# Half of x1's gate-stage products and its last three gate inputs stand beside c0's second gather tile

## The chip, the cores and the metric

The kernel runs on one core of one Trainium2 chip. The metric is the device time of one execution in microseconds (us), as the median of several runs. The engines of the core are named as in the profile: PE (TensorE matmul), PEld (its weight loads), DVE (VectorE), ACT (ScalarE), POOL (GpSimd) and SP (SyncE, which here only starts weight transfers).

## The reference, cut to what matters

Two blocks follow each other on 256 tokens of width 1024. The change lies in the first, which has two layers over two streams, the main stream x and the context ctx. One layer mixes tokens in three gated branches and then adds a mixture of looked-up experts:

```python
def _token_mix(h, lp, ang, kv_ctx):
    z = h @ lp["w_in"]
    cq, ckv, kr, zf, zp, zg = jnp.split(z, SPLITS, axis=-1)
    ...                                   # attention over 8 heads gives att
    y_a = att @ lp["w_oa"]
    y_b = _fourier_mix(zf) @ lp["w_ob"]
    y_c = _pool_mix(zp, lp["w_grp"], lp["pool_scale"]) @ lp["w_oc"]
    g = jax.nn.sigmoid((zg + lp["b_gate"]).astype(jnp.float32)).astype(h.dtype)
    g_a, g_b, g_c = jnp.split(g, N_BRANCH, axis=-1)
    return (g_a * y_a + g_b * y_b + g_c * y_c) @ lp["w_out"], (k, v)

def _peer(h, w_pq, peer_keys, peer_down, peer_up):
    ...                                   # 128 experts per token are chosen
    a = jnp.einsum("tkd,td->tk", peer_down[ee], hh)
    act = (gg * jax.nn.gelu(a)).astype(hh.dtype)
    return jnp.einsum("tk,tkd->td", act, peer_up[ee])
```

In the last layer the context is used only for its keys and values, so there the context has no mixing and no experts of its own.

## The kernel before, in words

The program calls its four passes c0, x0, x1 and c1: context or main stream, layer 0 or 1 (c1 is the context's keys and values for layer 1). The work is cut into stages such as ("gpre", "x1", 3, 0), and the functions `beside_x0`, `beside_c0` and `order` write the list of them by hand. Each engine walks the same list and issues its own part of every stage, so the list is the order on PE, DVE, ACT and SP alike. There is no scheduler; engines wait on semaphores only.

**The gathers.** Every pass but c1 looks up 128 experts for each token. A tile is 128 tokens (t = 0 or 1), and its 128 lookups go in 16 groups of 8. For one lookup POOL issues an indirect transfer of a 128 x 1024 tile from the table `peer_down` (L2504), DVE multiplies it with h and sums (L1984, `down`), the small gelu chain follows (DVE L1988 to L2003, ACT L1492), ACT writes a diagonal matrix (L1488, `diags`), POOL fetches the row of `peer_up` into the same buffer (L2504), and PE adds it up in four 128 x 128 by 128 x 512 passes (L992, `up`). For c0 the loop in `gather` does this: in group n, PE does `up(n - 1)`, DVE `down(n)`. The eight buffers `rows` are used in turn for a down row and an up row.

**Stages beside a gather.** A tile has 32 slots, two for each group. The stages in an even slot are run by PE ahead of `up(n - 1)`, by DVE between `down(n)` and `act_of(n)`, by ACT between `diags(n - 1)` and `tanh(n)`. In c0's second tile slot 32 is group 0, so slots 32 to 42 carry x1's branches (Fourier, pooling, queries) in groups 0 to 5, and slots 44, 46 and 48 carry ("gpre", "x1", dp, 0) in groups 6, 7 and 8. From slot 50 on, groups 9 to 15, the slots are empty. Runs of groups with empty slots are written as a hardware loop (`groups`), here six turns; POOL has its own loops, which the stages don't touch.

**Gates and branch products.** For each quarter dp of the 1024 columns and each branch j (0 attention, 1 Fourier, 2 pooling), `gpre` multiplies hT with a 1024 KB chunk of wG on PE (16 matmuls, L879) and ACT takes the tanh (L1449) into a place that `gate_at` names. `gate` with part 3 multiplies one 1024 KB chunk of wO with the branch outputs on PE (L899: 8 matmuls for j = 0, 4 for j = 1, 4 for j = 2), and DVE weights each with its gate and adds up (L1852, L1855, L1857) into mixT. The gates for dp = 0 to 2 of x1 are made beside the gathers of c0; those for dp = 3 and all the y products are made behind them.

**Between the gathers.** After c0's last tile nothing is gathered until x1's own experts are chosen. In that stretch stand: the norm of c1, the three gpre of dp = 3, the transposes of c1 (L697), its projection (L711), kv (L728, L736, L746), the heads of x1 (L846, L856, L869), the four gate stages, `out_` (L711), norm and transposes of x1, and the scoring (L922, L932).

**Weights.** SP starts the weight chunks in the order of the stages, into a ring of three buffers `wring`: a chunk is started when the chunk three before it has been used (`chunks`, L2309). Loads of a norm's gain stand in the same queue (L2315).

## Time and profile before

| | us |
|---|---|
| median of 3 runs | 4159.94 |
| lowest and highest of them | 4153.65, 4164.02 |
| the profiled execution, its own time | 4160.42 |
| its span in the profile | 4158.6 |
| c0's second gather tile (first `up` to the end of the last) | 1731.7 to 2103.2 |
| stretch without a gather, to the first expert row of x1 | 2103.2 to 2345.8 |

The times in a profile run from the start of the span. PE is busy for 83% of it, DVE for 56%, POOL for 36%, ACT for 23%. In the timeline a row gives start, duration, engine, line and operation, and in brackets how long the engine had been idle and what ended that. The program's fp32 matmuls appear as two records each, so 16 matmuls are x32.

### The profile page before, as it was taken

What the parts mean: (1) busy time and instruction counts of PE and PEld (TensorE: products, weight loads), DVE (VectorE), ACT (ScalarE), POOL (GpSimd) and SP (SyncE); (2) the same over time, 40 slices, a digit from 0 to 9 for tenths busy, and PEclk for the clock granted to TensorE, in tenths of its full rate; (3) what the DMA queues carried; (4) which work ended last, traced back from release to release, by engine and by line L of the source; (5) the groups of instructions that cost most, each with busy time, mean ns of one, the idle gap of its engine ahead of it and who ended that gap; (6) DMA issues with size and microseconds to landing.
All of it is one profiled execution on the core that took longest, in us unless ns stands there. A gap on an engine that the chain in (4) does not pass through costs nothing.

```text
span 4158.6 us, 43344 instructions
## 1 busy us (share of the span) xinstructions
PE 3469.0 (83%) x14118; PEld 2193.7 (53%) x14118; DVE 2323.3 (56%) x4974; ACT 950.0 (23%) x1940; POOL 1509.0 (36%) x1757
## 2 busy tenths in 40 slices
PE   6999787888895887777688677767789979999999
PEld 2576443354462452333255522222259869798898
DVE  2313876444557776444423666666546676565564
ACT  1301111121111111221121111111123453334443
POOL 0000566555555666566600277667730000000000
PEclk8999899999997998898899899989999989999999
DMA  6575899989897999999922599989965414545444
GB/s 269 192 267 194 316 391 367 363 313 345 343 359 292 388 394 360 333 375 374 352 102 96 209 388 400 381 335 379 399 255 186 177 55 165 185 175 179 143 175 153
DMA packets 273452, 1156.77 MB, mean 278 GB/s; under 512 B 30849, under 2 KB 31617, under 8 KB 234370
## 3 DMA queue, kind: packets, MB, share of 16 engines
q0 software_dynamic: 221184, 805.40, 51.0%
q1 hardware_dynamic: 52098, 349.23, 22.8%
q8 instruction: 90, 1.47, 0.1%
q14 instruction: 80, 0.66, 0.0%
HBM read 1153.47 MB, written 1.05 MB: 278 GB/s over the span
## 4 chain that ended last, share of the span: by engine, by line
PE 50%; DMA 19%; issue 11%; DVE 11%; POOL 7%; ACT 2%; POOLq 0%; SPq 0%; DVEq 0%; ACTq 0%
DMA rows<-in_peer_up,iup 11%; PE ps L992 11%; DMA rows<-in_peer_down,idown 7%; PE ps L1045 7%; PE ps L1047 7%; PE ps L1046 7%; POOL rows L2504 4%; PE ps L711 3%; PE ps L879 3%; PE ps L922 3%; POOL rows L2439 3%; DVE rows L1984 2%; PE ps L899 2%; DVE rows L1933 1%; PE ps L951 1%
## 5 line engine op out<-in xcount | busy, mean ns | idle before, releaser
L992 PE MATMUL ps<-rows,diag 128*128 128x512 f32 x2048 | 968.0, 631 | 292.6 <-DMA rows<-in_peer_up,iup 287.9
L992 PEld LDWEIGHTS ps<-rows,diag 128*128 128x128 f32 x2048 | 405.9, 202 | 835.7 <-issue 593.0
L1984 DVE CUSTOM_DVE_ANT_0 rows<-rows,ps 128x1024 f32<-128x1024 f32 x512 | 615.0, 1220 | 413.7 <-DMA rows<-in_peer_down,idown 405.7
L951 PE MATMUL ps<-rows,diag 128*128 128x512 f32 x1024 | 511.7, 625 | 209.8 <-DMA rows<-in_peer_up,iup 159.5
L2504 POOL DMA_INDIRECT rows<-in_peer_down,idown x512 | 488.6, 954 | 400.4 <-PE ps L992 281.9
L2504 POOL DMA_INDIRECT rows<-in_peer_up,iup x512 | 483.3, 944 | 257.0 <-issue 110.6
L951 PEld LDWEIGHTS ps<-rows,diag 128*128 128x128 f32 x1024 | 176.6, 191 | 542.8 <-DMA rows<-in_peer_up,iup 365.8
L1045 PE MATMUL ps<-hT_hi,w_hi 128*128 128x256 f32 x1600 | 452.4, 283 | 8.9 <-DVE hT_lo L2095 8.9
L1047 PE MATMUL ps<-hT_lo,w_hi 128*128 128x256 f32 x1600 | 453.1, 283 | 0.0
L1046 PE MATMUL ps<-hT_hi,w_lo 128*128 128x256 f32 x1600 | 451.3, 282 | 0.0
L1933 DVE CUSTOM_DVE_ANT_0 rows<-rows,ps 128x1024 f32<-128x1024 f32 x256 | 309.2, 1220 | 210.7 <-DMA rows<-in_peer_down,idown 209.1
L2568 POOL TENSOR_TENSOR ss<-nwt,minus_half 128x1 f32<-128x1 f32 x24 | 13.2, 550 | 1076.2 <-DVE nwt L1716 1076.2
L1488 ACT ACTIVATE diag<-ident,act 128x128 f32<-128x128 f32 x768 | 261.2, 395 | 459.7 <-PE ps L992 381.4
L2085 DVE TENSOR_TENSOR w_lo<-wring,w_hi 128x2048 fp32r<-128x2048 f32 x120 | 274.7, 2291 | 114.6 <-ACT w_hi L1559 113.6
L1045 PEld LDWEIGHTS ps<-hT_hi,w_hi 128*128 128x128 f32 x1600 | 306.1, 191 | 10.9 <-issue 10.8
L1046 PEld LDWEIGHTS ps<-hT_hi,w_lo 128*128 128x128 f32 x1600 | 305.6, 191 | 0.1
L1047 PEld LDWEIGHTS ps<-hT_lo,w_hi 128*128 128x128 f32 x1600 | 304.9, 191 | 0.0
L2439 POOL DMA_INDIRECT rows<-in_peer_down,idown x256 | 243.0, 949 | 122.9 <-issue 58.3
L2439 POOL DMA_INDIRECT rows<-in_peer_up,iup x256 | 242.5, 947 | 100.0 <-issue 72.0
L1559 ACT ACTIVATE w_hi<-wring 128x2048 fp32r<-128x2048 f32 x120 | 229.2, 1911 | 116.6 <-DMA wring<-in_wdn 86.5
L1492 ACT ACTIVATE th<-g 128x8 f32<-128x8 f32 x96 | 20.0, 208 | 833.5 <-DVE g L1943 539.5
L879 PE MATMUL ps<-hT,wring 128*128 128x256 f32 x928 | 207.8, 383 | 1.4 <-ACT hT L1304 1.4
(315 smaller groups left out, 4298.2 us busy)
## 6 DMA issues: line engine op xcount, KB each, us to landing
wring<-in_wgu SPq DMA_DIRECT2D x66, 1024.0 KB, 4.7
wring<-in_wdn SPq DMA_DIRECT2D x33, 1024.0 KB, 4.8
wring<-in_wG SPq DMA_DIRECT2D x29, 1024.0 KB, 7.9
rows<-in_wmod SPq DMA_DIRECT2D x27, 1024.0 KB, 7.9
wring<-in_wpq SPq DMA_DIRECT2D x24, 1024.0 KB, 4.9
rows<-in_wgu SPq DMA_DIRECT2D x22, 1024.0 KB, 4.8
wring<-in_wmod SPq DMA_DIRECT2D x21, 1024.0 KB, 7.2
rows<-in_peer_down,idown POOLq DMA_INDIRECT x768, 6.4
```

What stands on the lines that cost most here:

```text
L879: last = pe.matmul(b[:, dt * TOK:(dt + 1) * TOK], w[:, k * 256 + dt * P:k * 256 + (dt + 1) * P], hT[:, k, :], start=(k == 0), stop=(k == K ...
L951: ins = pe.matmul(ps[:, UPB + half, :], diag[:, j % DIAGS, :], rows[:, s, half * 512:(half + 1) * 512], start=(first and j == 0), stop=(la ...
L992: ins = pe.matmul(ps[:, UPB + half, :], diag[:, j % DIAGS, :], rows[:, j, half * 512:(half + 1) * 512], start=(first and j == 0), stop=(la ...
L1045: pe.matmul(out_, lh[l_at], rh[r_at], start=start, stop=False, skip_group_check=skip)
L1046: pe.matmul(out_, ll[l_at], rh[r_at], start=False, stop=False, skip_group_check=skip)
L1047: return pe.matmul(out_, lh[l_at], rl[r_at], start=False, stop=stop, skip_group_check=skip)
L1488: act.activation(diag[:, j % DIAGS, :], ident[:, :], ACT.Copy, scale=act8[:, j:j + 1]).then_inc(diag_ready, 1)
L1933: dve.tensor_tensor_reduce(out=rows[:, s, :], in0=rows[:, s, :], in1=h_ps, scale=1.0, scalar=0.0, op0=ALU.mult, op1=ALU.add, accum_out=a8[ ...
L1984: dve.tensor_tensor_reduce(out=rows[:, j, :], in0=rows[:, j, :], in1=h_ps, scale=1.0, scalar=0.0, op0=ALU.mult, op1=ALU.add, accum_out=a8[ ...
L2085: dve.tensor_tensor(W2_LO[c % SLOTS2], w, W2_HI[c % SLOTS2].bitcast(f32), ALU.subtract).then_inc(lo_ready, 1)
L2439: pool.indirect_dma_start(out=rows[:, s, :], out_offset=None, in_=table, in_offset=bass.IndirectOffsetOnAxis(ap=offs, axis=0)).then_inc(ro ...
L2504: pool.indirect_dma_start(out=rows[:, j, :], out_offset=None, in_=table, in_offset=bass.IndirectOffsetOnAxis(ap=offs[:, j:j + 1], axis=0)) ...
```

## The change

The change puts seven stages into the empty even slots 50 to 62 of c0's second tile. Four are new stages ybc: for one dp they make the y products of j = 1 and 2 and weight and add them on DVE. Three are the gpre of dp = 3, which stood behind the gather. Gate, for x1 alone, keeps only j = 0 and one addition. The chunk of wO is loaded in two halves, columns 1024 to 2047 for ybc and 0 to 1023 for gate. Since more gates are alive at once, those of dp = 3 go where already used ones were, and a new mark mixBC orders that: ACT waits for the ybc that has read the old gate before it writes the new one.

```diff
@@ beside_c0
     place(32, branches("x1") + [("gpre", "x1", dp, 0) for dp in range(3)], 2)
+    place(50, [("ybc", "x1", 0), ("ybc", "x1", 1), ("gpre", "x1", 3, 1), ("gpre", "x1", 3, 2), ("ybc", "x1", 3), ("ybc", "x1", 2), ("gpre", "x1", 3, 0)], 2)
@@ order
-    o += k[0:1] + [("gpre", "x1", 3, j) for j in range(3)] + k[1:] + flat(heads("x1") + mixing("x1") + scoring("x1"))
+    o += k + flat(heads("x1") + mixing("x1") + scoring("x1"))
@@ MARKS
+    "mixBC": (4, ["x1"]),
@@ chunks_of
     if name == "gate":
+        if st[1] == "x1":
+            return [("wO", (l, st[2], slice(None), slice(0, SLOT_W // 2)), SLOT_W // 2)]
...
+    if name == "ybc":
+        return [("wO", (l, st[2], slice(None), slice(SLOT_W // 2, SLOT_W)), SLOT_W // 2)]
@@ gate_at
             if dp == 3:
-                return (mb[:, 0:512], mb[:, 512:D], zA[0].rearrange("p t n -> p (t n)")[:, 0:512])[j]
+                return (junk[:, 512:D], h[0][:, 0, 512:D], h[0][:, 1, 512:D])[j]
@@ PE
+                branch_products(run, dp, [0] if run == "x1" else [0, 1, 2], 0)
...
+            def ybc(run, dp):
+                if dp == 0:
+                    at_evac(pe, ("Y", run))
+                    at_evac(pe, ("G", run))
+                branch_products(run, dp, [1, 2], 4)
@@ ACT, gpre
+                if run == "x1" and dp == 3:
+                    at_mark(act, "mixBC", run, (4, 1, 2)[j])
@@ DVE
             def gate(run, dp, part_):
...
+                if run == "x1":
+                    key = ("y", run, dp, 0)
+                    at_evac(dve, ("g", run, dp, 0))
+                    m = mixT[:, 2 * dp:2 * dp + 2, :]
+                    release(dve.scalar_tensor_tensor(m, pair_of(gate_at(run, dp, 0)), 1.0, pair_of(at_mm(dve, key)), ALU.add, ALU.mult), key)
+                    at_evac(dve, key)
+                    dve.tensor_tensor(m, m, pair_of(gate_at(run, dp, 1)), ALU.add).then_inc(mark["mixT"], 1)
+                    return
...
+            def ybc(run, dp):
+                kept = pair_of(gate_at(run, dp, 1))
+                tmp = pair_of(zA[0].rearrange("p t n -> p (t n)")[:, 0:512])
+                for j in (1, 2):
+                    key = ("y", run, dp, j)
+                    at_evac(dve, ("g", run, dp, j))
+                    release(dve.scalar_tensor_tensor(kept if j == 1 else tmp, pair_of(gate_at(run, dp, j)), 1.0, pair_of(at_mm(dve, key)),
+                                                     ALU.add, ALU.mult), key)
+                    at_evac(dve, key)
+                no = (0, 1, 3, 2).index(dp) + 1
+                dve.tensor_tensor(kept, kept, tmp, ALU.add).then_inc(mark["mixBC"], 1)
+                at_mark(dve, "mixBC", run, no)
```

On PE, at the end of c0's second tile and in the stretch behind it, the program before reads (L992 is `up`, L879 gpre, L697 and L711 c1's transposes and projection; the loop is shortened):

```order
L879 MATMUL ps<-hT,wring 128x256 x16
L992 MATMUL ps<-rows,diag 128x512 x16
L599 UNCONDITIONAL_BRANCH
...
L599 COMPARE_AND_BRANCH
L992 MATMUL ps<-rows,diag 128x512 x32
L648 MATMUL ps<-mrows,sel 128x512 x6
L879 MATMUL ps<-hT,wring 128x256 x48
L697 MATMUL ps<-ident,h_ctx 128x128 x16
L711 MATMUL ps<-wring,hT 128x416 x16
```

And changed, with its own line numbers (L1009 is `up`, L885 gpre, L910 the y products, L703 and L717 c1's):

```order
L885 MATMUL ps<-hT,wring 128x256 x16
L1009 MATMUL ps<-rows,diag 128x512 x16
L910 MATMUL ps<-YT,wring 128x256 x4
L910 MATMUL ps<-ypT,wring 128x256 x4
L1009 MATMUL ps<-rows,diag 128x512 x16
...
L885 MATMUL ps<-hT,wring 128x256 x16
L1009 MATMUL ps<-rows,diag 128x512 x32
L654 MATMUL ps<-mrows,sel 128x512 x6
L703 MATMUL ps<-ident,h_ctx 128x128 x16
L717 MATMUL ps<-wring,hT 128x416 x16
```

The loop is gone, a stage stands ahead of each of the last seven `up` pieces (the last of them the gpre in front of the closing x32), and the 48 matmuls between the norm's small ones and c1's transposes are gone.

On SP's queue, from the gain of a norm in that tile to c1's projection weights, before and changed:

```order
L2315 DMA gain<-in_norm_g 128x1024
L2309 DMA wring<-in_wG 128x2048 x3
L2309 DMA wring<-in_wA 128x1664 x2
L2309 DMA wring<-in_wukv 128x1024
L2309 DMA wring<-in_wO 128x2048 x4
```

```order
L2350 DMA wring<-in_wO 128x1024 x2
L2350 DMA wring<-in_wG 128x2048 x2
L2350 DMA wring<-in_wO 128x1024 x2
L2350 DMA wring<-in_wG 128x2048
L2356 DMA gain<-in_norm_g 128x1024
L2350 DMA wring<-in_wA 128x1664 x2
L2350 DMA wring<-in_wukv 128x1024
L2350 DMA wring<-in_wO 128x1024 x4
```

The four half chunks of ybc are new in the queue ahead of the gain of c1's norm, which now stands behind seven chunks.

## Rows read from the trace of the kernel before

**Rows 1.** The page, part 4: the chain that ended last, by engine
```profile
PE 50%; DMA 19%; issue 11%; DVE 11%; POOL 7%; ACT 2%; POOLq 0%; SPq 0%; DVEq 0%; ACTq 0%
```
**Rows 2.** That chain in c0's second tile and behind it: start us, us, what
```profile
1756.21 3.69 PE ps L992 x4
...
2049.86 3.67 PE ps L992 x4
...
2059.48 5.61 DMA rows<-in_peer_down,idown
2065.11 1.22 DVE rows L1984
...
2067.58 6.38 DMA rows<-in_peer_up,iup
...
2110.81 22.88 PE ps L879 x96
...
2204.05 27.88 PE ps L899 x128
```
**Rows 3.** Timeline of PE in c0's second tile
```profile
1756.21 15.70 PE L992 MATMUL ps<-rows,diag 128*128 128x512 f32 x32 [3.13 <-DMA rows<-in_peer_up,iup]
...
1833.82 16.17 PE L992 MATMUL ps<-rows,diag 128*128 128x512 f32 x32 [6.02 <-DMA rows<-in_peer_up,iup]
1849.83 7.07 PE L879 MATMUL ps<-hT,wring 128*128 128x256 f32 x32
...
1905.10 15.70 PE L992 MATMUL ps<-rows,diag 128*128 128x512 f32 x32 [1.86 <-DMA rows<-in_peer_up,iup]
1929.51 16.11 PE L992 MATMUL ps<-rows,diag 128*128 128x512 f32 x32 [8.72 <-DMA rows<-in_peer_up,iup]
...
2074.01 29.28 PE L992 MATMUL ps<-rows,diag 128*128 128x512 f32 x64 [8.48 <-DMA rows<-in_peer_up,iup]
```
**Rows 4.** Busy time by stretch, three groups of that tile
```profile
core 0: us, PE busy (x) PEld busy (x) DVE busy (x) ACT busy (x) POOL busy (x), PEclk, DMA share, GB/s
1858.40:1881.60 23.20, 21.17 (x65) 11.98 (x65) 10.16 (x19) 4.14 (x11) 15.16 (x17) 1.00 1.02 408
...
1929.50:1953.70 24.20, 16.16 (x33) 6.85 (x33) 10.38 (x20) 3.21 (x8) 15.08 (x18) 0.85 0.94 341
...
1756.20:1783.10 26.90, 20.45 (x56) 10.88 (x56) 14.07 (x40) 5.79 (x15) 17.54 (x21) 0.88 0.95 355
```
**Rows 5.** Timeline of DVE, from one group's last step to the next group's first
```profile
2050.69 0.17 DVE L2003 TENSOR_TENSOR act<-g,gates 128x8 f32<-128x8 f32 x1 [0.22 <-DVE g L1998]
2060.02 1.22 DVE L1984 CUSTOM_DVE_ANT_0 rows<-rows,ps 128x1024 f32<-128x1024 f32 x1 [9.16 <-DMA rows<-in_peer_down,idown]
```
**Rows 6.** Weight transfers from 2103 to 2280 us: count, KB each, us to landing
```profile
wring<-in_wO SPq DMA_DIRECT2D x4, 1024.0 KB, 4.8
...
wring<-in_wA SPq DMA_DIRECT2D x2, 832.0 KB, 4.4
...
wring<-in_wukv SPq DMA_DIRECT2D x1, 512.0 KB, 3.3
```
**Rows 7.** Timeline of PE between the gathers
```profile
2136.81 11.41 PE L711 MATMUL ps<-wring,hT 128*128 128x416 f32 x32 [1.40 <-ACT hT L1304]
...
2234.92 17.01 PE L711 MATMUL ps<-wring,shared 128*128 128x512 f32 x32
...
2252.91 14.00 PE L711 MATMUL ps<-wring,shared 128*128 128x512 f32 x32
...
2282.43 20.96 PE L922 MATMUL ps<-hT,wring 128*128 128x256 f32 x96 [0.99 <-ACT hT L1304]
```
**Rows 8.** Timeline of DVE between the gathers
```profile
2116.88 0.69 DVE L1774 TENSOR_TENSOR h_ctx<-h_ctx,ps 128x512 f32<-128x512 f32 x1
...
2209.61 0.69 DVE L1852 SCALAR_TENSOR_TENSOR shared<-h_in,ps 128x512 f32<-128x512 f32 x1 [1.07 <-PE ps L899]
...
2277.02 0.69 DVE L1774 TENSOR_TENSOR h_in<-h_in,ps 128x512 f32<-128x512 f32 x1
```

More of the change, by code:

```diff
@@ L890, in gate, with branch_products @@
                         at_evac(pe, ("pv", run, n))
-                    at_evac(pe, ("Y", run))
-                    at_evac(pe, ("G", run))
+                    if run != "x1":
+                        at_evac(pe, ("Y", run))
+                        at_evac(pe, ("G", run))
+                branch_products(run, dp, [0] if run == "x1" else [0, 1, 2], 0)
+            def branch_products(run, dp, js, k0):
                 w = chunk()
-                for j, ks in enumerate(([0, 1, 2, 3], [4, 5], [6, 7])):
+                for j in js:
+                    ks = ([0, 1, 2, 3], [4, 5], [6, 7])[j]
                     b = job(("y", run, dp, j))
@@ L898, in gate @@
                             rhs = attT[:, k, :] if j == 0 else (YT, ypT)[j - 1][:, (k % 2) * TOK:(k % 2 + 1) * TOK]
-                            last = pe.matmul(b[:, dt * TOK:(dt + 1) * TOK], w[:, k * 256 + dt * P:k * 256 + (dt + 1) * P], rhs,
+                            last = pe.matmul(b[:, dt * TOK:(dt + 1) * TOK], w[:, (k - k0) * 256 + dt * P:(k - k0) * 256 + (dt + 1) * P], rhs,
                                              start=(k == ks[0]), stop=(k == ks[-1]))
@@ L902, in gate @@
                 chunk_end()
+            def ybc(run, dp):
+                if dp == 0:
+                    at_evac(pe, ("Y", run))
+                    at_evac(pe, ("G", run))
+                branch_products(run, dp, [1, 2], 4)
             def out_(run, half, c):
@@ L1280, in _ @@
                        "start": start, "mod": mod, "norm": norm, "hT": hT_, "zA": zA_, "kv": kv, "zF": zF, "four": four, "q": q_, "att": att,
-                       "gate": gate, "gpre": gpre, "out": out_, "pq": pq, "gather": gather, "fb": fb, "fin": fin}
+                       "gate": gate, "gpre": gpre, "ybc": ybc, "out": out_, "pq": pq, "gather": gather, "fb": fb, "fin": fin}
             def run_stages(stages):
@@ L2280, in _ @@
             program = {"pre": pre, "hT2": hT2, "gu": gu, "dn": dn, "cout": cout, "qkv": qkv, "ao": ao, "post": post, "cin": cin, "ln": ln, "moba": moba,
-                       "start": start, "mod": mod, "norm": norm, "kv": kv, "q": q_, "att": att, "gate": gate, "out": out_, "route": route,
+                       "start": start, "mod": mod, "norm": norm, "kv": kv, "q": q_, "att": att, "gate": gate, "ybc": ybc, "out": out_, "route": route,
                        "gather": gather, "fin": fin, "final": final, "lower": lower}
@@ L2320, in per_stage @@
                     return int(args[1] == 2)
-                return {"mod": 2, "zA": 1, "zF": 1, "four": 2 - args[-1] if name == "four" else 0, "gate": 1, "gpre": 1, "out": 1}.get(name, int(name == "pq" and args[1] < 8))
+                return {"mod": 2, "zA": 1, "zF": 1, "four": 2 - args[-1] if name == "four" else 0, "gate": 1, "gpre": 1, "ybc": 1, "out": 1}.get(name, int(name == "pq" and args[1] < 8))
             for name, *args in STAGES:
```

## The prediction

> **What bounds the kernel now.** I read the chain that ended last first, since it says whose time counts: half of it is PE's, a fifth is transfers, DVE and issue have 11% each [rows 1]. Then I followed the same chain through the two places that the change touches, because its shares mix stages with different limits.
>
> In c0's second tile the chain goes round once for each group: PE takes the first rows, that frees a buffer, a down row is fetched (5.61 us), DVE takes it (1.22), an up row is fetched (6.38), and only then can PE begin the next group [rows 2]. The timeline of PE shows what that leaves. An empty group is some 16 us of `up` and then 8 to 9 us of idle, ended by the up row [rows 3]. From 1905.10 to 2074.01 there are seven such groups, so one takes 24.13 us. So PE has a hole in each, and work in it is paid only where it outlasts the hole or slows the round trip.
>
> Behind the gather there is no such cover. The three gpre take 22.88 us of the chain and the four gate stages 27.88 us, all PE's [rows 2]. The stretch ends with the scoring, which the next gather waits for; all that is taken out of it comes off the total, if nothing else is late instead.
>
> **Part 1, the three gpre.** They are 48 matmuls, 22.88 us of chain. Not all of it comes back, because they cover the norm of c1. DVE begins the first h piece that c1's transposes wait for at 2116.88 [rows 8], six microseconds into the gpre. What is late next is that norm. How long the way from that piece to a running matmul is, the same code shows on x1: the piece begins at 2277.02 [rows 8], the matmuls behind the transposes at 2282.43 [rows 7], 5.41 us later, with a PE that had stood idle before, as it now will here. So c1's projection starts at 2116.88 + 5.41 = 2122.29 where it now starts at 2136.81 [rows 7]. **Saved: 14.5 us.** Its bounds are 22.9 (the norm would not count) and 11.5 (the projection loses 3 us to a low clock, below). Its weights are not late: SP's queue has them behind the last gpre's chunk, and the ring frees their buffers in groups 13 and 14, before the gather ends. The same holds for the gain of c1's norm, which goes out when the gpre of group 12 is done, some 100 us before DVE wants it.
>
> **Part 2, the gate stages.** The 64 matmuls take 27.88 us; j = 0 is 8 of every 16, so 13.94 us remain. **Saved: 13.9 us.** The end is as before: PE waits for DVE's product and one addition. For one quarter DVE now has one product and one addition of 0.69 us each [rows 8] against 3.5 us of PE, so it keeps up. The weights shrink with the work: three half chunks are in the ring early, the fourth starts when the first is used, 3.5 us into the stage, and is wanted at 10.5; a whole chunk took 4.8 us [rows 6]. The first chunk of `out_` starts 7 us into the stage and is wanted at about 16.
>
> **Part 3, what the gather pays.** PE gets four ybc of 8 matmuls (27.88 / 128 x 16 records = 3.5 us each) and three gpre of 7.07 [rows 3], 35 us of work in seven holes of 8 to 9 us. The nearest rows are groups 6 to 8 of the same tile, which have a gpre and one 1024 KB chunk each: three of them take 1905.10 - 1833.82 = 71.28, or 23.76 each, less than the 24.13 of an empty one [rows 3]. The windows say why. With the gpre the granted clock is 1.00 (the 2.4 GHz level throughout), without it 0.85 [rows 4]: behind 8.7 us of idle the first row of `up` takes 3.67 us in the chain [rows 2]. So a gpre gives back some 0.4 to 0.9 us, although the transfers are slower beside its chunk. A ybc leaves 5 us of hole. After 3.13 us of idle the clock had already fallen once, the first row took 3.69 [rows 2, 3], so I give it no gain, and 0.3 us of loss for its chunk. Three gpre at -0.7 and four ybc at +0.3 make **-1 us**. The bounds for the seven: -0.9 each (23.20 against 24.13), -6; and +2.8 each, as in the group at 1756.20, which had two chunks at once and took 26.90 [rows 4], +19.6.
>
> DVE gets three operations of 0.69 us in a ybc, 2.1 us and some waiting, between `down` and `act_of`. Queued behind them are the last two small steps, on which ACT's diagonals and so PE's next-but-one piece depend. They are covered: DVE sits idle for 9.16 us after these steps [rows 5], and the diagonals are held back by PE's own progress, not by DVE. The products that ybc waits for are made at the start of PE's hole, while DVE is still at its down rows. ACT's new wait on mixBC stands ahead of its tanh for the gelu; the ybc it names lies one group back or more, so it costs nothing. If that cover is gone, it is the third rival below. POOL issues what it issued. That the six loop turns become straight code I cost at nothing: groups 0 to 8 are straight code and no slower.
>
> The transfers are nearer to their limit. The tile takes 4 x 512 + 2 x 832 + 512 = 4224 KB more [rows 6], 4.3 MB: ybc's half chunks of wO, and c1's weights that now come early. But never more than 1024 KB in a group, as in groups 6 to 8. These move 408 GB/s at a share of 1.02, an empty one 341 [rows 4]. The tile has that room by the rows. The Trainium skill, DMA: Bandwidth & Descriptors, section Where 436 GB/s comes from, speaks against the change: it puts the limit from HBM at some 358 GB/s for a core, by which 4.3 MB more would take 12 us. The trace disagrees with it in the group at 408, so the sum goes by the rows.
>
> **The sum.** 14.5 + 13.9 + 1 = 29.4 us off 4160.4 of the profiled execution (span 4158.6 and 1.8 around it) is **4131.0**. That execution lies 0.5 us above the median of the runs, which is nothing here.
>
> **The rivals.**
> *The transfers are full.* Each extra byte lengthens the tile at the rate of an empty group: 4.3 MB at 341 GB/s is 12.7 us, which gives 4160.4 - 28.4 + 12.7 = 4144.7. For it: the share is 0.94 even in empty groups, and the group with two chunks took 2.8 us more. Against it: three groups with a chunk each took less time, not more. The skill's 358 GB/s, above, would be this case.
>
> *The clock falls in the stretch behind.* c1's transposes now follow 7 us of idle. In the present trace the first half of `out_` took 17.01 us and the second 14.00 for the same work [rows 7], after a short idle. One such loss is 3 us (4134), a projection wholly at the lower level would lose its own 11.4 us again (4142). Against the latter: x1's scoring came up at full pace directly behind its transposes [rows 7].
>
> *A stage is serial with its group.* Were PE's stage, DVE's three operations and the way to the diagonals in the round trip, each stage would cost its own length: 4 x (3.5 + 2.1) + 3 x 7.07 = 43.6 us, the total 4160.4 - 28.4 + 43.6 = 4175.6, slower than before. It decides from 28.4 / 7 = 4.1 us for each stage. Against it speak the gpre groups (7.07 us of work, no loss) and DVE's 9.16 us of idle; for it only that no c0 group of this tile has had work of PE and DVE in a chain with the gelu.
>
> *The change does less than it says.* If c1's norm were later than it looks, or another wait took the gates' place, one of the two savings halves: 4138.
>
> **How the numbers follow.** The forecast, 4125 to 4137, has 0.66; full transfers 0.12; a low clock 0.09; less than it says 0.07; the serial stage 0.03; more gain in the gather than I count (down to 4160.4 - 28.4 - 6.3 = 4125.7, and some of the norm's cover) 0.03. The range 4122 to 4146 takes in all but the serial stage, the heaviest end of full transfers and a wholly low clock on top of another loss. A measurement of this kernel can tell about 0.3%, 12.5 us, from no change. Faster by more than that is below 4147.5, which all cases but the serial stage and the worst of the transfers reach: 0.93. Within it 0.05, slower 0.02.
>
> **What would show it.** In the changed profile PE should reach c1's projection 19 us after the end of the last `up` (33.5 now), hold 64 records of y products between the heads and `out_` in 14 us, and show groups 9 to 14 of the tile at 23 to 25 us. If these groups stand at 26 with DMA at a share of 1.0 throughout, the transfers were full. If PE waits there for diagonals of ACT, the stage is serial. A projection above 12 us means the clock. The prediction is wrong if groups cost over 2 us more each, or if PE waits for a chunk in the gate stages.

## The result, and the profile after the change

The change made the kernel faster: 4136.62 us against 4159.54 us, medians of 7 runs each on one chip, ratio 0.9948 with a 95% interval of 0.9934 to 0.9961. That is 21.6 us off at the ratio, 16 to 27.5 by the interval. Forecast were 29.4 us and 4131.0; the result lies inside the range of 4122 to 4146, 5.6 us from the forecast. The gain of 29.4 us that was forecast lies just above the interval of the measured one. The profiled execution took 4140.86 us, its span 4138.7 against 4158.6. The page, part 1, busy time of the engines after the change:

```profile
PE 3472.4 (84%) x14118; PEld 2195.5 (53%) x14118; DVE 2322.5 (56%) x4974; ACT 950.1 (23%) x1940; POOL 1518.8 (37%) x1757
```

The work was only moved, so these totals say little. Where the time came from stands in the timelines. First PE in c0's second tile (start us, us, engine and line, operation, count, and in brackets the idle time before and what ended it):

```profile
1880.20 14.22 PE L1009 MATMUL ps<-rows,diag 128*128 128x512 f32 x32 [0.85 <-DMA rows<-in_peer_up,iup]
...
1902.72 5.42 PE L1009 MATMUL ps<-rows,diag 128*128 128x512 f32 x12 [1.39 <-DMA rows<-in_peer_up,iup]
...
1917.73 1.89 PE L910 MATMUL ps<-YT,wring 128*128 128x256 f32 x8
1919.45 1.89 PE L910 MATMUL ps<-ypT,wring 128*128 128x256 f32 x8
1927.13 15.79 PE L1009 MATMUL ps<-rows,diag 128*128 128x512 f32 x32 [5.79 <-DMA rows<-in_peer_up,iup]
...
1952.10 16.95 PE L1009 MATMUL ps<-rows,diag 128*128 128x512 f32 x32 [5.72 <-DMA rows<-in_peer_up,iup]
...
1976.80 5.42 PE L1009 MATMUL ps<-rows,diag 128*128 128x512 f32 x12 [0.84 <-DMA rows<-in_peer_up,iup]
...
2001.02 5.40 PE L1009 MATMUL ps<-rows,diag 128*128 128x512 f32 x8 [2.30 <-DMA rows<-in_peer_up,iup]
...
2028.91 16.10 PE L1009 MATMUL ps<-rows,diag 128*128 128x512 f32 x32 [6.50 <-DMA rows<-in_peer_up,iup]
...
2055.24 16.59 PE L1009 MATMUL ps<-rows,diag 128*128 128x512 f32 x32 [6.77 <-DMA rows<-in_peer_up,iup]
2071.66 7.07 PE L885 MATMUL ps<-hT,wring 128*128 128x256 f32 x32
2080.00 27.86 PE L1009 MATMUL ps<-rows,diag 128*128 128x512 f32 x64 [1.26 <-DMA rows<-in_peer_up,iup]
```

The holes that had 8 to 9 us of idle [rows 3] now hold the moved products (3.6 us for a ybc, 7.07 for a gpre). From the start of one `up` to the next the seven groups take 24.4, 25.0, 24.7, 24.2, 27.9, 26.3 and 24.8 us, in the order ybc 0, ybc 1, gpre, gpre, ybc 3, ybc 2, gpre. That is 177.3 us where the same seven took 168.9 [rows 3]: **+8.4**, and the two groups of ybc 3 and ybc 2 have 6.0 of it. The two groups ahead of the seven took 2.4 us less and the closing 64 records 1.4 less (27.86 against 29.28, PE comes warm, that is at the full granted clock, out of a gpre). "The fifth group" and the like count from here on among these seven. Busy time in four of the groups (columns as in [rows 4]):

```profile
1902.70:1927.10 24.40, 17.72 (x48) 8.96 (x48) 11.45 (x25) 3.63 (x10) 16.34 (x19) 0.94 1.02 408
...
1976.80:2001.00 24.20, 21.18 (x64) 11.99 (x64) 10.58 (x21) 4.36 (x12) 15.41 (x19) 1.00 0.99 378
2001.00:2028.90 27.90, 19.68 (x48) 9.42 (x48) 12.79 (x27) 3.63 (x10) 17.14 (x21) 0.89 1.00 377
2028.90:2055.20 26.30, 19.56 (x48) 9.83 (x48) 12.02 (x24) 3.42 (x9) 15.71 (x19) 0.89 0.95 354
```

The group that moved most bytes a second (408) is not the long one. SP's transfers around the fifth and sixth group:

```profile
1998.75 0.33 SPq L2350 DMA_DIRECT2D wring<-in_wG  x1
1999.12 0.43 SPq L2356 DMA_DIRECT2D gain<-in_norm_g  x1
2022.44 26.39 SPq L2350 DMA_DIRECT2D wring<-in_wA  x2
```

The last row holds two transfers, at 2022.44 and 2048.50. A gpre frees its chunk at the end of its hole, a ybc in the middle of its own, so the last wG chunk (1024 KB), the gain (512 KB) and the first wA chunk (832 KB) fall into the fifth group, 2.4 MB. Then PE between the gathers, same columns:

```profile
2107.79 1.13 PE L654 MATMUL ps<-mrows,sel 2*128 2x512 f32 x4
...
2122.19 3.48 PE L703 MATMUL ps<-ident,h_ctx 128*128 128x128 f32 x16 [10.48 <-DVE h_ctx L1793]
2126.61 11.41 PE L717 MATMUL ps<-wring,hT 128*128 128x416 f32 x32 [0.95 <-ACT hT L1321]
...
2193.98 14.05 PE L910 MATMUL ps<-shared,wring 128*128 128x256 f32 x64 [0.78 <-ACT shared L1321]
2209.61 1.12 PE L654 MATMUL ps<-mrows,sel 2*128 2x512 f32 x2 [1.58 <-DVE shared L1871]
2210.66 15.68 PE L717 MATMUL ps<-wring,shared 128*128 128x512 f32 x32
...
2257.22 23.25 PE L939 MATMUL ps<-hT,wring 128*128 128x256 f32 x96 [0.99 <-ACT hT L1321]
```

PE now waits 10.48 us for DVE's norm of c1 and then begins the projection 18.8 us after the gather's last `up` (2126.61 - 2107.79), where it took 33.6 (2136.81 - 2103.22). The gate products are 64 records in 14.05 us, with no wait for a chunk, and 15.6 us (2209.61 - 2193.98) stand where 29.5 stood. The projection is at the full pace of 11.41 us. x1's scoring takes 23.25 us against 20.96 [rows 7], 2.3 us given back at a lower clock.

In one sum, after minus before, in these two executions: seven groups +8.4, the two ahead -2.4, the closing block -1.4, to c1's projection -14.8, the gates -13.8, the first half of `out_` -1.3 (15.68 against 17.01) and -0.3 in the small matmuls ahead of it, x1's norm +0.4, the scoring +2.3, what follows it +0.2. With +0.1 between projection and gates that puts x1's first expert row 22.7 us earlier, and 2.8 are lost in the rest of the program, which the change does not touch: -19.9 in the span.

### The profile page after: what moved, and what is told of

It reads as the page before. It is cut to its first block, busy times and chain, and to the rows that moved or that the text cites. A ratio compares the mean times of both kernels' runs of the same rounds, so it can differ in the third digit from the quotient of the medians.

```text
span 4138.7 us, 43250 instructions
## 1 busy us (share of the span) xinstructions
PE 3472.4 (84%) x14118; PEld 2195.5 (53%) x14118; DVE 2322.5 (56%) x4974; ACT 950.1 (23%) x1940; POOL 1518.8 (37%) x1757
## 3 DMA queue, kind: packets, MB, share of 16 engines
q1 hardware_dynamic: 52674, 349.23, 22.9%
## 4 chain that ended last, share of the span: by engine, by line
PE 49%; DMA 18%; issue 12%; DVE 10%; POOL 8%; ACT 2%; POOLq 0%; SPq 0%; DVEq 0%; ACTq 0%
DMA rows<-in_peer_up,iup 11%; PE ps L1009 11%; PE ps L1062 7%; PE ps L1063 7%; PE ps L1064 7%; DMA rows<-in_peer_down,idown 6%; POOL rows L2545 6%; PE ps L717 3%; PE ps L939 3%; PE ps L885 3%; POOL rows L2480 2%; DVE rows L2025 2%; PE ps L968 1%; PE ps L910 1%; DVE rows L1974 1%
## 5 line engine op out<-in xcount | busy, mean ns | idle before, releaser
L1009 PE MATMUL ps<-rows,diag 128*128 128x512 f32 x2048 | 967.7, 631 | 262.5 <-DMA rows<-in_peer_up,iup 256.4
L1009 PEld LDWEIGHTS ps<-rows,diag 128*128 128x128 f32 x2048 | 404.7, 202 | 803.6 <-issue 535.2
L885 PE MATMUL ps<-hT,wring 128*128 128x256 f32 x928 | 206.0, 380 | 1.4 <-ACT hT L1321 1.4
```

Source lines behind the costliest of these rows:

```text
L885: last = pe.matmul(b[:, dt * TOK:(dt + 1) * TOK], w[:, k * 256 + dt * P:k * 256 + (dt + 1) * P], hT[:, k, :], start=(k == 0), stop=(k == K ...
L1009: ins = pe.matmul(ps[:, UPB + half, :], diag[:, j % DIAGS, :], rows[:, j, half * 512:(half + 1) * 512], start=(first and j == 0), stop=(la ...
```

## The experiments

Of the three terms two fit within 0.3 us. Open was the third: why do the seven groups take 177 us, when three gpre groups before them take 23.76 each? The theories that the runs were to tell apart:

- **B, bytes.** Each chunk lengthens the gather by its bytes over the DMA rate. (The expectations have B, above all the 2.4 MB of the fifth group, together with G as T.)
- **C, the clock.** A short ybc leaves PE idle long enough that the next `up` starts slow, and so every row behind it is late.
- **G, the gain.** SP issues the transfer of c1's gain right behind the last wG chunk, and it stands in the way of rows.
- **S, straight code.** The loop turns written out cost something.
- **P, the phase**, formed on runs 1 to 8, run 6 above all: the cost depends on when in the group a chunk starts. At the end of its hole PE waits for up rows. A chunk that SP starts early in the hole comes in among these. One that starts when `up` has begun comes in beside down rows, which are paced by PE itself.

Group times in us, from one start of `up` to the next, worked out from each run's timeline of PE; ratios against the kernel before on the same chip, with 95% interval. Runs 1 to 4 had one chip (before 4160.32 us), 5 to 8 another (4251.71), 9 to 11 a third job (4239.02), 12 a fourth (4253.98).

```
                          groups                                     sum    ratio
before (shown)            24.4 24.1 24.3 23.7 24.4 23.9 24.2         168.9
after  (shown)            24.4 25.0 24.7 24.2 27.9 26.3 24.8         177.3  0.9948 [0.9934, 0.9961]
1  after again            25.0 25.9 25.1 22.7 27.4 26.9 25.5         178.5  0.9943 [0.9920, 0.9965]
2  gain early             24.3 25.4 24.9 23.2 27.6 26.9 24.5         176.7  0.9952 [0.9929, 0.9976]
3  ybc twice              23.3 23.4 23.0 22.4 29.3 22.8 22.9         167.1  0.9917 [0.9880, 0.9954]
4  before, straight code  23.6 25.2 24.3 23.6 24.1 24.5 24.0         169.4  1.0004 [0.9992, 1.0016]
5  before, warm           23.9 22.9 23.9 23.4 24.9 23.6 23.4         166.1  0.9992 [0.9974, 1.0010]
6  before, one load       26.5 27.5 27.1 29.4 26.7 26.6 27.0         190.7  1.0055 [1.0038, 1.0072]
7  gain early, late wA    27.9 25.6 23.6 22.8 27.5 24.8 23.9         176.0  0.9949 [0.9922, 0.9975]
8  as 7, ybc twice        24.8 23.5 25.1 23.5 28.0 22.7 23.5         170.9  0.9928 [0.9900, 0.9956]
9  chunk late             24.4 23.8 24.8 22.2 28.6 24.7 23.7         172.1  0.9932 [0.9902, 0.9962]
10 warm, chunk early      24.4 23.0 25.0 23.9 30.0 25.2 23.9         175.3  0.9945 [0.9928, 0.9963]
11 late, reordered        25.2 24.7 23.9 23.9 24.7 23.5 23.0         168.9  0.9942 [0.9927, 0.9957]
12 twice, reordered       24.7 24.0 23.4 23.3 25.2 22.8 24.1         167.5  0.9940 [0.9923, 0.9957]
```

The groups of different jobs are not quite alike. In runs 1 to 4, and in the traces of before and after, a chunk freed by a gpre left 0.6 to 2.3 us ahead of the next `up`. In runs 5 to 12 many such chunks, and some freed by a ybc, left 4 to 6.5 us behind the start of `up` (in run 7, 1934.26 against 1928.08). Why is not known.

**1. The changed kernel again.** No edit.

> The changed kernel once more, to see which group times repeat. In the profile shown, the seven groups with a new stage took 24.4, 25.0, 24.7, 24.2, 27.9, 26.3 and 24.8 us from first up to first up, against 24.13 for each before, +8.4 in all. If the bunched transfers cause the loss (theory T: the last wG chunk, the gain of c1's norm and c1's first wA chunk, 2.4 MB, fall into one group), the 27.9 repeats within 0.7 us, and so does the 26.3. If it is chance in the row transfers, the two long groups move elsewhere.

Measured 4138.48 us. The two long groups are there again (27.4, 26.9), and the sum is 1.2 us from the first trace. They are no accident of one execution, and a difference of some 2 us between two sums is the scatter.

**2. The gain early.** SP loads the gain of c1's norm ahead of ybc 0's chunk:

```diff
-                if name == "norm":
+                if name == "ybc" and args == ["x1", 0]:
+                    load_gain(A["norm1_g"][1])
+                if name == "norm" and args == ["c1", 0]:
+                    pass
+                elif name == "norm":
```

> The gain of c1's norm is loaded ahead of ybc's first chunk, about where the kernel before had it, and no longer beside the last wG chunk. T: the group of 27.9 us loses 2 to 3 us, the others stay; the end of the last up comes 2 to 3 us earlier. Rival C (the clock and PE's hole: a ybc of 3.5 us leaves 5 us of idle, the clock falls, and PE's stage no longer pays for itself): nothing changes, 27.9 stays.

Measured 4138.91 us, groups 27.6 and 26.9: nothing moved. G falls, and with it that half of T.

**3. Each ybc product twice.** The second pass starts from zero again, so the output is the same; the ybc lasts 7.2 us like a gpre, and frees its chunk as late.

```diff
-                    for dt in range(2):
+                    for dt in [0, 1] * (2 if k0 else 1):
```

> Each ybc makes its products twice over in the same banks (the first pass is overwritten), so PE has 7 us of work in the hole, as with a gpre, and the same transfers. Clock theory C: the granted clock in the four ybc groups goes from about 0.90 to 0.97 or more, the first row of up takes 2.0 instead of 3.8 us, and each of these groups gets about 1 us shorter, 4 us in all. Transfer theory T: the four groups stay within 0.4 us each, for the round trip then waits for rows. Serial theory: each gets 3.5 us longer, 14 us in all.

More work of PE made the groups shorter: 167.1 against 178.5, and all but the fifth are at 22.4 to 23.4. That is 11.4 us, where C had forecast 4 and the serial theory 14 us of loss. The timeline of PE in this run, the sixth group and its end, and under it SP's transfer of c1's second weights:

```profile
2021.52 5.42 PE L1009 MATMUL ps<-rows,diag 128*128 128x512 f32 x12 [1.15 <-DMA rows<-in_peer_up,iup]
...
2036.12 3.62 PE L910 MATMUL ps<-YT,wring 128*128 128x256 f32 x16
2039.57 3.62 PE L910 MATMUL ps<-ypT,wring 128*128 128x256 f32 x16
2044.36 14.30 PE L1009 MATMUL ps<-rows,diag 128*128 128x512 f32 x32 [1.17 <-DMA rows<-in_peer_up,iup]
```

```profile
2043.22 0.33 SPq L2350 DMA_DIRECT2D wring<-in_wA  x1
```

The chunk leaves at 2043.22, 1.1 us before `up`, where after's left at 2048.50 and `up` began at 2055.24 (below). PE's `up` then takes 14.30 us (2055.24: 16.59), and the up row ahead of it, in the chain of waits, 5.97 us:

```profile
2038.34 5.97 DMA rows<-in_peer_up,iup
```

The busy time of its second group shows that bytes alone don't lengthen a group: 406 GB/s and 23.40 us.

```profile
1923.50:1946.90 23.40, 21.18 (x64) 11.97 (x64) 12.69 (x25) 3.42 (x9) 15.47 (x18) 1.00 1.01 406
```

The run was not yet decisive, as it changes the clock and the chunk's start together. Of its total, 4119.35 us (span 4117.2 against 4140.0 in run 1), 13.5 us stand at the end of the tile (first small norm matmul at 2094.95 against 2108.45). The rest came in stretches with the same code, and the interval is 0.9880 to 0.9954, so the total is not to be read as the worth of the edit.

**4. Straight code alone.** Before, with seven empty steps in the table, which makes the six loop turns straight code:

```diff
+    place(50, [("nop", "x1")] * 7, 2)
```

> The kernel before with seven empty stages in slots 50 to 62, so that the six loop turns on PE, DVE and ACT become straight code and nothing else changes. If straight code costs something (instruction loading), the seven groups of 24.13 us grow, by 1.2 us each if it were the whole of the loss. I expect no change: 24.1 within 0.3 us each, total within 3 us of the kernel before.

Measured 4161.10 us, ratio 1.0004, groups 169.4 (one of its eight times, 11011.73 us, stands apart, unexplained; the median hardly feels it). S falls; the prediction's zero for it holds.

**5. Work without transfers.** Before, with 16 unused matmuls of the gpre's shape in each of the seven holes:

```diff
+            def warm(run, n):
+                b = job(("warm", n))
+                for dt in range(2):
+                    for k in range(KT):
+                        last = pe.matmul(b[:, dt * TOK:(dt + 1) * TOK], ident[:, :], hT[:, k, :], start=(k == 0), stop=(k == KT - 1))
+                release(last, ("warm", n))
```

> The kernel before, with 16 matmuls of gpre's shape in each of the seven empty groups, on ident and hT, their result unused and no transfer added. Clock theory C: PE's hole is filled, the first row of up takes 2.0 instead of 3.7 us, and each of the seven groups falls from 24.1 to about 22.8, the tile gets 8 to 10 us shorter and the whole kernel with it. Serial theory: each group grows by up to 7 us. If the clock does not count, 24.1 stays.

The sum is 166.1, 0.4 us per group below the 168.9 of the trace of before (another chip), and the total is 4251.73 against 4251.71. C had forecast groups of 22.8 and 8 to 10 us of the total. Timeline of PE and one window:

```profile
1955.02 15.64 PE L993 MATMUL ps<-rows,diag 128*128 128x512 f32 x32 [3.02 <-issue]
1970.50 7.07 PE L1284 MATMUL ps<-hT,ident 128*128 128x256 f32 x32
1977.93 14.00 PE L993 MATMUL ps<-rows,diag 128*128 128x512 f32 x32 [0.36 <-DMA rows<-in_peer_up,iup]
```

```profile
1977.90:2001.80 23.90, 20.91 (x64) 12.08 (x64) 10.40 (x20) 3.20 (x9) 16.53 (x20) 1.00 0.97 355
```

Without idle ahead `up` takes 14.00 us, with 3.02 us of it 15.64. But PE then waits longer for its next rows, so a group wins 0.4 us of these 1.6. C is real and small, on its own. In four of the seven groups the granted clock was 1.00, in the other three 0.93.

**6. A transfer without work.** Before, with one 1024 KB chunk and two tiny matmuls in each hole, so that the chunk is freed, and the next one started, at the very start of the hole:

```diff
+            def load(run, n):
+                chunk()
+                for key in (("load", n, 0),):
+                    b = job(key)
+                    ended(pe.matmul(b[:, 0:16], ident[:, :], ident[:, 0:16], start=True, stop=True), key)
+                    release(pe.matmul(b[:, 0:16], ident[:, :], ident[:, 0:16], start=True, stop=True), key)
+                chunk_end()
```

> The kernel before, with one more wG chunk of 1024 KB loaded and freed in each of the seven empty groups, and no work beside two tiny matmuls. This is the price of a chunk with a cold PE. By C and T together a chunk costs about 1.0 us a group (24.1 to 25.1), 7 us in all, which the warm PE of a gpre group hides. If full transfers bound the tile, each grows by 1 MB at 341 GB/s, 3.1 us, 21 us in all; if transfers are free, 24.1 stays.

The expectation fell: total +23.4 us on 4251.71 (ratio 1.0055), groups of 27.2 in the mean. The 3.1 us a group and 21 in all that it had named for full transfers are what came. Timeline of PE and one window:

```profile
1984.33 16.43 PE L995 MATMUL ps<-rows,diag 128*128 128x512 f32 x32 [10.62 <-DMA rows<-in_peer_up,iup]
2000.59 0.29 PE L1286 MATMUL ps<-ident 128*128 128x16 f32 x2
2011.39 16.55 PE L995 MATMUL ps<-rows,diag 128*128 128x512 f32 x32 [10.29 <-DMA rows<-in_peer_up,iup]
```

```profile
1956.90:1984.30 27.40, 16.81 (x36) 7.48 (x36) 10.59 (x22) 3.42 (x9) 15.30 (x18) 0.75 0.94 345
```

PE waits 10.3 to 10.6 us for its up row, where before it waited 8 to 9. In the fourth group (29.4) SP started the gain as well, right behind the chunk. The six groups with a chunk alone take 26.9 us, 2.8 more than the 24.13 of an empty one [rows 3]; the chunk's 1,048,576 bytes over the 341 GB/s of an empty group [rows 4] are 3.1 us. The rate is that of an empty group too (345), so here B alone would do. The Trainium skill, DMA: Bandwidth & Descriptors, section Issuing engines are not separate DMA queues, says that transfers issued by different engines run on the same 16 DMA engines and interleave; run 6 agrees, with these 2.8 us a chunk. Yet the gpre groups [rows 3] have the same chunk for nothing. What differs, beside PE's clock, is its start: there SP starts it when the gpre has ended, 1 to 2 us ahead of `up`, and here 10.5 to 12.7. From this came P.

**7. Late weights.** Run 2, and SP holds c1's first weights until c0's rows are done:

```diff
+                    if name == "zA" and args == ["c1", 0]:
+                        at_mark(sp, "fin", "c0", 2)
```

> The change with the gain early and with c1's wA and wukv held back on SP until c0's last tile is done, so that these transfers leave the gather's last groups. T: the last ybc group (26.3, 26.9 and 26.9 us in three runs) falls to about 25 and the one with the last gpre by some 0.5; the long one (27.4 to 27.9) by 1, since wA's first chunk starts within it. c1's projection still starts on time, for wA lands some 9 us before it is wanted. Total 3 us less than the change. C alone: the groups stay.

The sixth and seventh groups fell to 24.8 and 23.9, from 26.9 and 25.5 in run 1, as expected: the chunk of wA is what they had paid. The fifth stayed at 27.5, where 1 us less was expected, so neither the gain nor wA makes it long. The first took 27.9, which no theory had; in this trace two chunks of 1024 KB start within it (1934.26 and 1948.36), but in run 6 two do as well (1935.92 and 1946.19) and it took 26.5. The total, 0.9949, is that of the change and not 3 us less: the sum is only 1.3 us under 177.3. c1's projection begins on time, 19.0 us after the gather's last `up` (2150.77 - 2131.75).

**8. Run 7 with each product twice.** Its edit is run 3's on top of run 7's:

```diff
-                    for dt in range(2):
+                    for dt in [0, 1] * (2 if k0 else 1):
```

> The last one with ybc's products made twice, so that PE is warm in all seven groups. C and T: the groups take 23 to 23.5 us but for the long one, the whole lies 3 us under the run with the products twice alone (4119.4), near 4116. If late wA is nothing beside a warm PE, 4119.

The sum is 170.9, between runs 3 and 7; the first and third groups (24.8, 25.1) are above the 23 to 23.5 expected. The fifth stands at 28.0 with PE warm, no gain and no wA in it. Total 4224.80, 0.9928, not below run 3's ratio of 0.9917.

**9. The chunk late, PE unchanged.** The test of P against C: after, where SP waits for the first row of the next `up` before it starts a chunk whose buffer a ybc has freed. PE's work and idle time stay.

```diff
+                    if before in ybc_rows:
+                        sp.wait_ge(upp_done, ybc_rows[before])
```

> The change, with SP starting the chunk that a ybc frees only when PE has done the first row of the next up piece; PE's work and all bytes stay. Phase theory P, formed on the runs so far: a chunk started early in PE's hole gets in front of the up rows for which PE waits, one started late, as behind a gpre or behind products made twice, comes in beside up and costs little. P: the four ybc groups fall to 24 to 24.7 us each (from 24.4 to 27.9, the one behind the last wG chunk to about 26), the seven from 177 to about 171, total 5 to 7 us under the change. Clock theory C: PE is as idle as before, so nothing changes, 177. Bytes alone (T): nothing changes.

The sum is 172.1 (P had 171), 5.2 below the changed kernel's first trace and 6.4 below run 1 (both on another chip), at the same bytes and with PE as cold. But of the 5.2 only 2.1 lie in the four ybc groups, the rest in the gpre groups, of which P says nothing. The fifth group did not fall to 26. The total, 0.9932 with 0.9902 to 0.9962, cannot be told from the change's. SP and PE in this run around the sixth group:

```profile
2071.02 0.33 SPq L2354 DMA_DIRECT2D wring<-in_wA  x1
```

```profile
2042.81 16.30 PE L1011 MATMUL ps<-rows,diag 128*128 128x512 f32 x32 [4.59 <-DMA rows<-in_peer_up,iup]
2058.95 1.89 PE L911 MATMUL ps<-YT,wring 128*128 128x256 f32 x8
2060.67 1.89 PE L911 MATMUL ps<-ypT,wring 128*128 128x256 f32 x8
2067.54 15.70 PE L1011 MATMUL ps<-rows,diag 128*128 128x512 f32 x32 [4.97 <-DMA rows<-in_peer_up,iup]
```

The chunk leaves 3.5 us behind the start of `up`, and PE had waited 4.97 us. In the changed kernel, SP around that group:

```profile
2048.50 0.33 SPq L2350 DMA_DIRECT2D wring<-in_wA  x1
```

It left 6.7 us ahead of `up` (2055.24), and PE had waited 6.77. In the chain of waits of the changed kernel the up row in that hole takes 8.12 us against 6.38 [rows 2]:

```profile
2047.07 8.12 DMA rows<-in_peer_up,iup
```

**10. PE warm, the chunk early.** The counterpart: 8 unused matmuls behind each ybc, when its chunk is already freed.

```diff
                 branch_products(run, dp, [1, 2], 4)
+                b = job(("warm", dp))
+                for k in range(KT):
+                    last = pe.matmul(b[:, 0:TOK], ident[:, :], hT[:, k, :], start=(k == 0), stop=(k == KT - 1))
+                release(last, ("warm", dp))
```

> The change, with 8 matmuls more behind each ybc, on ident and hT and unused, after the chunk has been freed. PE is as warm as with the products made twice, but the chunk still starts early in the hole. P: the seven groups stay near 175 to 177 us, less 0.4 us for each warm piece. C: they fall to 167, as in the run with the products made twice.

The sum is 175.3, where P had 175 to 177 less 0.4 for each warm piece, and C 167. PE and SP around the same group:

```profile
2050.93 14.29 PE L1013 MATMUL ps<-rows,diag 128*128 128x512 f32 x32 [2.94 <-DMA rows<-in_peer_up,iup]
...
2068.51 3.62 PE L922 MATMUL ps<-hT,ident 128*128 128x256 f32 x16
2076.12 15.70 PE L1013 MATMUL ps<-rows,diag 128*128 128x512 f32 x32 [4.00 <-DMA rows<-in_peer_up,iup]
```

```profile
2068.70 0.33 SPq L2354 DMA_DIRECT2D wring<-in_wA  x1
```

The chunk left 7.4 us ahead of `up`, PE still had to wait 4.00 us in spite of the extra work, and the group took 25.2. In the fifth group too the chunk was early (6.4 us ahead). In the first and second it was not. PE and SP there:

```profile
1949.09 14.00 PE L1013 MATMUL ps<-rows,diag 128*128 128x512 f32 x32 [3.53 <-issue]
```

```profile
1930.63 20.99 SPq L2354 DMA_DIRECT2D wring<-in_wG  x2
1977.76 24.30 SPq L2354 DMA_DIRECT2D wring<-in_wO  x2
```

The chunk that ybc 0 freed left at 1951.30 (the second of the first row) and that of ybc 1 at 1977.76, 2.2 and 5.7 us (`up` at 1972.06) behind the start of `up`. So the edit gave an early chunk in two of the four groups only, and that the sum came out as P had it is in part luck: the unexplained fifth group took 30.0. What the runs say of P has to be read group by group. "Early" is 5.5 us and more ahead of `up`, "late" 1.2 us ahead to 6.2 behind; PE is "cold" where a ybc leaves it idle as in the change, "warm" where the hole is filled. In brackets the run (the first values are the trace of the change):

```
                    second group                            sixth group
cold, chunk early   25.0 25.9 (1) 25.4 (2) 25.6 (7)         26.3 26.9 (1) 26.9 (2)
cold, chunk late    23.8 (9) 24.7 (11)                      24.7 (9)
cold, no chunk                                              24.8 (7)
warm, chunk early                                           25.2 (10)
warm, chunk late    23.4 (3) 23.5 (8) 23.0 (10) 24.0 (12)   22.8 (3)
warm, no chunk                                              22.7 (8)
```

In the sixth group an early chunk of 832 KB costs 1.6 to 2.4 us and a late one nothing, with PE cold or warm, and the clock is worth 1.1 to 2.1. Runs 9 and 10, from one job, are the cold late and the warm early corner; by PE's work alone the warm one should be the shorter, and it is 0.5 us longer. In the second group the start is worth 0.3 to 2.1 us. In the first it is not seen outside run 7 (24.3 to 25.0 early, 24.4 and 25.2 late in runs 9 and 11), and in the fifth not at all (28.6 in run 9). The other corners stand in different jobs, one trace each, so these are sizes and no more.

**11. Chunk late, gain early, another order.** As 2 and 9, with the seven steps in the order ybc 0, ybc 1, gpre, gpre, ybc 2, gpre, ybc 3:

```diff
-    place(50, [("ybc", "x1", 0), ("ybc", "x1", 1), ("gpre", "x1", 3, 1), ("gpre", "x1", 3, 2), ("ybc", "x1", 3), ("ybc", "x1", 2), ("gpre", "x1", 3, 0)], 2)
+    place(50, [("ybc", "x1", 0), ("ybc", "x1", 1), ("gpre", "x1", 3, 1), ("gpre", "x1", 3, 2), ("ybc", "x1", 2), ("gpre", "x1", 3, 0), ("ybc", "x1", 3)], 2)
```

> Late chunks as in the run before last, the gain of c1's norm early, and the stages in the order ybc 0, ybc 1, gpre 1, gpre 2, ybc 2, gpre 0, ybc 3, so that a half chunk is started where the change starts the last wG chunk and its group takes 27.9 us. P: the seven groups near 169 us, the total 8 to 10 us under the change, 31 to 33 under the kernel before. If the long group comes from that chunk wherever it is fetched, it moves one group ahead; if it comes from the expert rows of that group, it stays in place.

The sum is 168.9, and the long fifth group is gone (24.7):

```profile
2026.81 5.40 PE L1011 MATMUL ps<-rows,diag 128*128 128x512 f32 x8 [1.86 <-DMA rows<-in_peer_up,iup]
...
2051.47 15.47 PE L1011 MATMUL ps<-rows,diag 128*128 128x512 f32 x32 [5.02 <-DMA rows<-in_peer_up,iup]
```

Neither of the two alternatives came: the last wG chunk, which now starts in front of the fourth group (2001.64 against `up` at 2002.93), took its length nowhere (23.9), and the fifth group, with the same expert rows, is short. The seven groups then pay what they paid before, 168.9, for 35 us more of PE's work and all the bytes. The order ends with a ybc and no longer with a gpre, so the closing block goes back to 29.82 us from 27.86. The total, 0.9942, cannot be told from the change's 0.9948, where 8 to 10 us less were forecast.

**12. Products twice, gain early, the new order.** The edits of 2, 3 and 11's order together; of 9's wait nothing.

```diff
-    ... ("ybc", "x1", 3), ("ybc", "x1", 2), ("gpre", "x1", 3, 0)], 2)
+    ... ("ybc", "x1", 2), ("gpre", "x1", 3, 0), ("ybc", "x1", 3)], 2)
```

> The version to beat both kernels: the gain of c1's norm early, the stages in the order of the run before, and ybc's products made twice, which fills PE's hole and starts each chunk late without a wait on SP. By P the seven groups take 163 to 167 us (177 in the change), none over 25; the total lies 12 to 18 us under the change and 35 to 40 under the kernel before, a ratio of 0.991 to 0.992.

The sum is 167.5, at the upper end of the 163 to 167 expected, and the fifth group 25.2, where none was to be over 25. The total missed its 0.991 to 0.992: 0.9940 with 0.9923 to 0.9957. It beats the kernel before, as the change does, and not provably the change.

## Why the prediction was right, and where it was off

**Right: what bounds the kernel.** PE has a hole in each group and none behind the gather. 36.8 us of the chain's PE work (22.88 and 13.94) went into the holes, and 28.6 (14.8 and 13.8) came off the stretch behind.

**Right: the three gpre.** Forecast -14.5, measured -14.8. The norm of c1 is late next, as said: PE waits 10.48 us for DVE's last h piece. x1's way from piece to matmul carried over, and the 22.9 us that the chain seemed to offer were not to be had.

**Right: the gate stages.** Forecast -13.9, measured -13.8, 14.05 us of products without a wait for a chunk.

**Off: what the gather pays.** The mis-sized term is part 3's four ybc at +0.3 each; they took +0.3, +0.8, +3.8 and +2.2. The three gpre, put at -0.7 each, took +0.6, +0.1 and +0.6. Instead of -1 us the seven groups cost +8.4, of which the groups ahead of them (half chunks in them now) and the closing block gave back 3.8: +4.6 at the end of the tile. Both bounds, -6 and +19.6, held it. So the total is close to the forecast although this term is 5.6 us off. The reasoning that was off is the choice of the nearest row. Groups 6 to 8 of the tile have a chunk each for nothing, and I took the chunk for cheap. Their gpre lasts till the hole's end and so holds the next chunk back (and keeps PE warm). A ybc frees its buffer in the middle of the hole (1921.37, the hole ends at 1927.13). From this the prediction's "never more than 1024 KB in a group" is wrong too: 2.4 MB start in or just ahead of the fifth. What the runs show of the excess: of the sixth group's +2.2 an early start is worth 1.6 to 2.2 (run 9, and run 7 without the chunk), and the second group falls to 23.8 and 24.7 with its chunk late (runs 9 and 11). The +3.8 of the fifth and the +1.3 of the three gpre are not explained by it. The half chunk of ybc itself, the only cost I counted, was the wrong one: the transfer that a ybc lets start is that of a later stage. (The first row of 3.67 us, read in part 3 as behind 8.7 us of idle, stands behind 8.19; nothing hangs on it.)

**The rivals.** *Full transfers* (12.7 us, total 4144.7) was nearest to what the tile did, but not by its mechanism: run 3's group moves 406 GB/s in 23.40 us, and run 9's sixth group has the same chunk as the change's in 1.6 us less. In run 6 alone it fits. By the same row the 358 GB/s of the Trainium skill (DMA: Bandwidth & Descriptors, named in the prediction) do not bound a group. *The clock falls behind the gather*: only at the scoring, 2.3 us, and `out_` won 1.3. *A serial stage* would have cost 43.6 us, and PE never waited for ACT's diagonals. *Less than it says*: both savings are whole. *Straight code at nothing* is right (run 4).

**Still open.** The fifth group takes 27.4 to 30.0 us in every run with the change's order, whatever the gain, the clock, wA, or the start of wA (runs 1 to 3 and 7 to 10), and 24.7 and 25.2 where the order of the steps is another (runs 11 and 12). In all the long ones the last wG chunk starts right in front of it, but the same chunk in front of the fourth group costs nothing there. That the expert rows of this very group are slow fits in part: it is the longest of the seven in runs 5 (24.9) and 12 (25.2) as well. What in the sequence is slow was not separated; it is 3.8 us of the 8.4.

The totals are too coarse for the tile. From the second group ahead of the seven to the end of the closing block the kernel before takes 244.9 us, the change 249.5, run 9 245.9, run 10 248.9, run 11 244.3 and run 12 243.9. So runs 11 and 12 should gain 5 to 6 us on the change, a ratio of 0.9935, which lies in their intervals, but so does the change's 0.9948. Run 5 (243.4) should gain 1.5 us on the kernel before, and its interval holds both that and no gain at all. Whether a gather that ends earlier gives its whole gain to the total was not settled.

## What to carry to other kernels

A prefetch beside a gather can be priced by when it starts: the same 832 KB cost some 2 us when they left while PE waited for rows, and nothing when they left with `up`. So find who frees its buffer and whether the critical engine is waiting for rows just then; if it is, try to hold the prefetch back until the first rows are in. Check in the trace that an edit moved the transfer it was to move, in each group: run 10's did in two of four. The nearest row of a trace carries its own phase and clock, so a shorter stage in the same place is not that row less some work. When work leaves a serial stretch, look for what it had covered: here the norm kept 8 of 22.9 us, and the same code elsewhere in the trace gave its length to 0.3 us.

## What was not expected of the hardware

A chunk of 1 MB that had cost nothing in three groups cost 2.8 us each in six (run 6). The DMA share was 0.94 and the rate 341 and 345 GB/s in an empty group and in one of run 6, while a gpre group with the same chunk ran at 1.02 and 408 [rows 4]; so a share of 0.94 did not mean that no more could be moved, and what holds an empty group at 341 is not shown. With PE's holes filled the granted clock went from 0.85 to 0.93 or 1.00 in a group, but this gave 0.4 us a group, too little for the total to show (run 5). And the unchanged kernel took 4160 us on one chip and 4239 to 4254 in the other jobs, 2% apart, four times the effect that was measured: only ratios on one chip mean anything here.
